# A mixture-of-experts stage on one core: one token tile's heads, then the other's, tokens in PSUM, routing in four parts

## What is computed

```
q = (xblk @ w_query).reshape(B, TOKEN_BLOCK, N_PEER_HEADS, 2, SUBKEY_DIM)      # 8 heads
s = einsum('bthpd,hpnd->bthpn', q, sub_keys)                                   # 2 x 128 keys
vals, idx = top_k(s, 16)
cand = vals[..., 0, :, None] + vals[..., 1, None, :]                           # 256 candidates
top_s, pos = top_k(cand, 16);  eidx = take_along_axis(cand_idx, pos)           # 16 of 16,384 experts
g = softmax(top_s)
h = einsum('btd,bthkd->bthk', xblk, expert_u[eidx])                            # a dot product of 1024
act = gelu(h) * g
y = einsum('bthk,bthkd->btd', act, expert_v[eidx])
```

## Time and profile before

| | |
|---|---|
| median of 3 runs | 3719.93 us (3708.38 to 3737.20) |
| the profiled execution | 3748.34 us, span 3746.5 us |
| busy in the span | PE 86%, PEld 69%, DVE 64%, ACT 39%, POOL 33% |
| POOL, 512 gathers each of u and v rows | 548.1 and 557.0 us busy, mean 1070 and 1088 ns |
| DVE, 512 dot products | 615.6 us busy, mean 1223 ns |
| HBM read | 932.73 MB, 249 GB/s over the span |
| expert stages (first to last u gather) | 284.9 to 1046.5 us and 1318.0 to 2084.9 us |

### The profile page before, as it was taken

How to read it: one execution, slowest core, us unless ns; L and a number is a source line. 1 busy time by engine, 2 the same in 40 slices (tenths; PEclk the granted TensorE clock), 3 DMA queues, 4 the chain that set the end, 5 groups by cost and what they waited for, 6 DMA issues and landing times. The chain is left out here.

```text
span 3746.5 us, 50783 instructions
## 1 busy us (share of the span) xinstructions
PE 3234.4 (86%) x18906; PEld 2588.8 (69%) x18906; DVE 2395.2 (64%) x4712; ACT 1457.6 (39%) x2874; POOL 1238.6 (33%) x1211
## 2 busy tenths in 40 slices
PE   6997788777789968887877799999999999999999
PEld 6894344443268944444432599888999998898899
DVE  6776666655557555655666565877666656767565
ACT  3642222222236412222221344565554444565543
POOL 1306677777623056776777200010000000000000
PEclk7998899988899988888988899999999999999999
DMA  7669999999976489999999654434355554334354
GB/s 294 212 222 349 380 366 384 382 365 358 331 280 207 141 335 360 368 373 361 377 357 361 228 183 152 147 119 141 130 170 185 183 183 141 130 135 135 131 185 163
DMA packets 258290, 937.14 MB, mean 250 GB/s; under 512 B 29312, under 2 KB 30720, under 8 KB 257792
## 3 DMA queue, kind: packets, MB, share of 16 engines
q0 software_dynamic: 161280, 587.27, 41.6%
q1 hardware_dynamic: 96768, 346.62, 27.1%
HBM read 932.73 MB, written 1.05 MB: 249 GB/s over the span
## 5 line engine op out<-in xcount | busy, mean ns | idle before, releaser
L695 PE MATMUL M<-rows,diag 128*128 128x512 f32 x2048 | 984.7, 638 | 350.9 <-ACT diag L919 257.8
L695 PEld LDWEIGHTS M<-rows,diag 128*128 128x128 f32 x2048 | 413.4, 205 | 882.1 <-issue 873.1
L268 DVE TENSOR_TENSOR w_low<-ring,w_high 128x1024 fp32r<-128x1024 f32 x560 | 685.9, 1228 | 415.0 <-ACT w_high L260 412.4
L1210 DVE CUSTOM_DVE_ANT_0 rows<-rows,attn 128x1024 f32<-128x1024 f32 x512 | 615.6, 1223 | 463.6 <-DMA rows<-in_expert_u_dram,expert 414.3
L287 PE MATMUL G<-x_high,w_high 128*128 128x256 f32 x2576 | 764.5, 297 | 50.0 <-DVE w_low L268 17.0
L290 PE MATMUL G<-x_high,w_low 128*128 128x256 f32 x2576 | 741.4, 288 | 0.0
L260 ACT ACTIVATE w_high<-ring 128x1024 fp32r<-128x1024 f32 x560 | 588.6, 1054 | 349.0 <-PE G L287 324.2
L289 PE MATMUL G<-x_low,w_high 128*128 128x256 f32 x2448 | 706.1, 288 | 0.0
L412 POOL DMA_INDIRECT rows<-in_expert_v_dram,expert x512 | 557.0, 1088 | 279.4 <-issue 129.6
L412 POOL DMA_INDIRECT rows<-in_expert_u_dram,expert x512 | 548.1, 1070 | 302.1 <-issue 154.5
L287 PEld LDWEIGHTS G<-x_high,w_high 128*128 128x128 f32 x2576 | 507.6, 197 | 63.6 <-issue 38.4
(11 more groups left out here) (360 smaller groups left out, 4779.8 us busy)
## 6 DMA issues: line engine op xcount, KB each, us to landing
ring<-in_stream_dram SPq DMA_DIRECT2D x654, 512.0 KB
ada_ring<-in_ada_stream_dram POOLq DMA_DIRECT2D x80, 512.0 KB, 4.9
rows<-in_ada_stream_dram POOLq DMA_DIRECT2D x16, 512.0 KB
rows<-in_expert_u_dram,expert POOLq DMA_INDIRECT x512
rows<-in_expert_v_dram,expert POOLq DMA_INDIRECT x512
const<-in_const_dram SPq DMA_DIRECT2D x1, 1096.5 KB, 11.2
x<-in_x_dram SPq DMA_DIRECT2D x1, 1024.0 KB, 5.4
out_dram<-x SPq DMA_DIRECT2D x8, 128.0 KB, 3.5
```

The lines of the kernel that those rows point to most:

```text
L268: dve.tensor_tensor(T["w_low"][:, part, :], T["ring"][:, place.slot(chunk, slots), :], T["w_high"][:, part, :].bitcast(F32), ALU.subtract) ...
L695: mm = pe.matmul(M[:, 2 * t + half, :], T["diag"][:, n % 4, :], T["v_rows"][:, n % SLOTS, half * 512:(half + 1) * 512], start=(h == 0 and ...
L1210: dve.tensor_tensor_reduce(row, row, T["x_tok"][:, t, :], 1.0, 0.0, ALU.mult, ALU.add, T["hid"][:, r, k:k + 1]).then_inc(sem["u_used"], 1)
```

## The change

It has six parts. Rounds now go `t, h = divmod(r, PEER_HEADS)`: all heads of tile 0, then all of tile 1. The tokens are transposed into PSUM and read from there: tile 0 in banks 2 and 3 of `M`, which tile 1's sum needs only from round 8 on, and tile 1 (after round 6) in two banks of `G`; the product becomes a `scalar_tensor_tensor` with an accumulator. `route` is cut into four parts behind products 2, 4, 6 and 8. `weigh` comes one product after its group's last in place of two. The queries of head r + 2 are done within round r, for r = 0 to 5. And y of tile 0 is finished in rounds 8 to 10.

```
-QUERY_AFTER = {(0, 5): 0, (0, 11): 1, (1, 1): 2, (1, 7): 3, (1, 12): 4}
-QUERY_COPIES = {(0, 2): 0, (0, 3): 1, (1, 1): 2, (1, 2): 3, (1, 3): 4}
+QUERY_AFTER = {0: 0, 2: 1, 4: 2, 6: 3, 8: 4}
+ROUTE_AFTER = {2: 0, 4: 1, 6: 2, 8: 3}
...
+    x_turned = (M[:, 2:4, :], G[:, G_XT % GB:G_XT % GB + 2, :])
+    x_tok = [tile.rearrange("p a b -> p (a b)") for tile in x_turned]
...
+            def turn_x(t):
+
+                if t:
+                    for n in range(2):
+                        bank_free(pe, g_free, G_XT + n)
+                for q in range(KD):
+                    mm = pe.transpose(x_turned[t][:, q // 4, q % 4 * P:(q % 4 + 1) * P],
+                                      xm[:, q, t * P:(t + 1) * P], ident)
+                    if t and q % 4 == 3:
+                        mm.then_inc(g_full, 1)
+                if t == 0:
+                    mm.then_inc(sem["x_turned"], 1)
...
             def add_experts(r):
 
-                h, t = divmod(r, TT)
+                t, h = divmod(r, PEER_HEADS)
...
-                    if h + 2 < PEER_HEADS and (t, k) in QUERY_AFTER:
-                        query_part(h + 2, QUERY_AFTER[t, k])
-                    if r == ROUNDS - 1 and k == SUB:
+                    if k in QUERY_AFTER and r + 2 < PEER_HEADS:
+                        query_part(r + 2, QUERY_AFTER[k])
+                    if r == PEER_HEADS and k == TOPK // 2:
                         turn_y(0)
+                if r == PEER_HEADS - 2:
+                    turn_x(1)
+                if opening and r == PEER_HEADS + 2:
+                    next_mean(0)
...
             for r in range(ROUNDS):
-                for at in range(r * TOPK, (r + 1) * TOPK, SUB):
-                    if at == ROUNDS * TOPK - SUB:
+                for j in range(TOPK // SUB):
+                    diagonals(r * TOPK + j * SUB)
+                    if r + 2 < PEER_HEADS and j in (1, 2):
+                        query_part(r + 2, 2 * j - 2)
+                        query_part(r + 2, 2 * j - 1)
+                    if j == 2 and r + 1 < ROUNDS:
+                        expert_softmax(r + 1)
+                    if r == PEER_HEADS and j == 0:
+                        copy_y(0)
+                    if r == PEER_HEADS + 2 and j == 0:
                         next_x(0)
...
+                if r + 2 < PEER_HEADS:
+                    query_part(r + 2, 4)
...
-                    dve.tensor_tensor_reduce(row, row, T["x_tok"][:, t, :], 1.0, 0.0, ALU.mult, ALU.add,
-                                             T["hid"][:, r, k:k + 1]).then_inc(sem["u_used"], 1)
-                    if k % SUB == 1 and n > SUB:
+                    dve.scalar_tensor_tensor(out=row, in0=row, scalar=1.0, in1=x_tok[t], op0=ALU.mult,
+                                             op1=ALU.mult, accum_out=T["hid"][:, r, k:k + 1]
+                                             ).then_inc(sem["u_used"], 1)
+                    if k % SUB == 0 and n:
                         weigh(n // SUB - 1)
-                    if k == SUB - 1 and r + 1 < ROUNDS:
-                        route(r + 1)
-                    if r == ROUNDS - 1 and k == TOPK - SUB - 1:
-                        add_y(0)
+                    if k in ROUTE_AFTER and r + 1 < ROUNDS:
+                        route_part(r + 1, ROUTE_AFTER[k])
```

More of the change, by code:

```diff
@@ L722, in _ @@
             first_queries()
-            for t in range(TT):
-                for half in range(2):
-                    g = G_XT + 2 * t + half
-                    bank_free(pe, g_free, g)
-                    for q in range(4):
-                        mm = pe.transpose(G[:, g % GB, q * P:(q + 1) * P],
-                                          xm[:, 4 * half + q, t * P:(t + 1) * P], ident)
-                    mm.then_inc(g_full, 1)
-            queries(1)
             pe.wait_ge(sem["std_ready"], F_NORM + 1)
             pe.wait_ge(sem["ada_read"], len(parts))
-            for h in range(PEER_HEADS):
-                for t in range(TT):
-                    add_experts(h * TT + t)
-            if opening:
-                next_mean(0)
+            pe.wait_ge(sem["o_ready"], HEADS)
+            turn_x(0)
+            queries(1)
+            for r in range(ROUNDS):
+                add_experts(r)
             turn_y(1)
@@ L891, in _ @@
                                    scale=scale1[:, 1, k:k + 1]).then_inc(sem["xm_ready"], 1)
-            def queries(h):
-                for j in range(5):
-                    query_part(h, j)
             def query_part(h, j):
@@ L935, in _ @@
                 first_queries(t)
[L936 to L939 removed]
+            for j in range(5):
+                query_part(1, j)
             expert_softmax(0)
             for r in range(ROUNDS):
[L942 to L952 removed]
+                for j in range(TOPK // SUB):
[8 more added lines that the diff above has]
+                    if r == PEER_HEADS + 2 and j == 0:
+                        next_x(0)
+                if r + 2 < PEER_HEADS:
+                    query_part(r + 2, 4)
                 if opening and r == 4:
@@ L1151, in route, with route_part @@
             def route(r):
-                h, t = divmod(r, TT)
-                evacuated(dve, g_free, g_scores(h, t))
+                for part in range(4):
+                    route_part(r, part)
+            def route_part(r, part):
+                t, h = divmod(r, PEER_HEADS)
                 val, idx, idxf, rest = T["val"], T["idx"], T["idxf"], T["rest"]
-                for p in range(2):
+                cand, top, pos = T["cand"], T["top"][:, r, :], T["pos"]
+                if part < 2:
+                    p = part
+                    evacuated(dve, g_free, g_scores(h, t))
                     s = T["key_score"][:, h, (2 * t + p) * P:(2 * t + p + 1) * P]
@@ L1200, in products @@
             def products(r):
-                t = r % TT
+                t, h = divmod(r, PEER_HEADS)
                 if r == 0:
-                    for g in range(2 * TT):
-                        evacuated(dve, g_free, G_XT + g)
+                    dve.wait_ge(sem["x_turned"], 1)
+                if r == PEER_HEADS:
+                    dve.wait_ge(g_full, G_XT + 2)
                 for k in range(TOPK):
@@ L1253, in _ @@
             for r in range(ROUNDS):
-                if not opening and r == ROUNDS - 1:
+                if not opening and r == PEER_HEADS:
                     dve.wait_ge(nxt["par_loaded"], 16)
@@ L1258, in _ @@
                 products(r)
+                if r == PEER_HEADS + 1:
+                    add_y(0)
+                if not opening and r == PEER_HEADS + 2:
+                    next_low(0)
                 if opening and r == 2:
@@ L1261, in _ @@
             weigh(ROUNDS * TOPK // SUB - 1)
-            if not opening:
-                next_low(0)
             add_y(1)
@@ L2494, in program @@
             att = sb1("attn", KD * S)
-            T1["attn"], T1["x_tok"] = part(att, 0, KD, S), part(att, 0, TT, D)
+            T1["attn"] = part(att, 0, KD, S)
             gates = sb1("gates", 2 * KD * S)
```

87 lines of the change are left out of this document (39 added, 48 removed).

## The result

| | median us | lowest to highest | runs | profiled run, span | clock |
|---|---|---|---|---|---|
| before | 3716.8 | 3692.4 to 3742.6 | 9 | 3746.5 | 0.929 |
| changed | 3692.1 | 3687.6 to 3696.9 | 9 | 3690.8 | 0.943 |

The ratio is 0.9939 with a 95% interval of 0.9914 to 0.9964: about 23 us came, where 88 were forecast. The profiled run of the kernel before (3748.3 us) was 31.5 us above this median, so the spans differ by more (55.7 us) than the medians.

What follows compares the result with a forecast made beforehand. GpSimd's gather rounds were taken as the bound. Gains of 110.7 us in the last ten rounds, less 26.9 in the first six, plus 4.5 at the ends, gave 88 us: median 3632 us, range 3580 to 3705.

Steps and rivals of the forecast that it cites:

- rival B: GpSimd's gathers: the stretch stays, from their own descriptor writing or the product's output; gain 18 us, 3702 us; chance 0.14.
- Bound by GpSimd's rounds: Last ten rounds: GpSimd sets the pace, each round 39.9 us of gathers plus 4.5 of stretch and 3.2 of waits.
- The gathers stretch because of the second SBUF input, and x in PSUM removes it: Last ten rounds: gathers lengthen during dot products reading two SBUF tensors; with x in PSUM, 44.7 and 44.2 us go.
- Routing in four ... I leave 1.0 of 3.2 us a round: Last ten rounds: splitting the 10.5 us routing block and earlier weights cut GpSimd's waits from 3.2 to 1.0 us a round.
- the queries' loop: Rounds 0 to 5: late score copies delay VectorE's routing; a round lies between 46.7 and 54.3 us.
- Transfers next at 410 GB/s, 417.7 us: Last ten rounds: transfers become the bound, 40.9 us a round plus 1.0 of waits, 417.7 us for 319 gathers.
- Rival A: Last ten rounds: transfers sustain only 388 GB/s, not 410; 438.6 us for 319 gathers, gain 46 us, 3674 us; chance 0.17.
- Queries moved, 49 us a round: First six rounds: a head's query work within one round makes it 49 us, 305.3 us in all; 26.9 us lost.
- Rival C: Rounds 0 to 5: the loop through routing and score copies takes over, 60 us a round; 44 us slower, 3764; chance 0.09.
- C's sign: Rounds 0 to 5: in the profile after, VectorE would be idle before the first MAX8 of a round.
- Ends of the stage, 4.5 us: Tail of each expert stage: tile 0's squares or copies and half a mean square leave, about 2.3 us a layer.
- TensorE's clock at nothing: Last ten rounds: TensorE needs 27.5 us of 42 at 2.4 GHz, so clock switching was costed at nothing.

Runs made afterwards that it cites:

- v eight behind: Changed kernel with v gathers running eight behind the u gathers instead of four: 3597.8 us on chip 3 (ratio to before 0.9908), 3753.1 us on chip 4 (1.0107).

## Why the prediction was wrong

The median, 3692, lies inside the range, near its upper edge (3705) and rival B's number (3702). That is luck: B was not what happened, the forecast 88 us were 23, and two errors of opposite sign are in them, 66.6 us too much in the last ten rounds and 38.0 us too little in the first six.

**Bound by GpSimd's rounds:** right. Where signals were prompt (chip 3, v eight behind), 58 us more stretch made the last ten rounds 50 us longer, and the waits gave the rest (11.7 to 1.0 us).

**The gathers stretch because of the second SBUF input, and x in PSUM removes it:** right. 947 ns a gather, the stretch 45.1 to 2.2 us, dot products of 1.22 us; with x back in SBUF it returned on all three chips where that ran (56.6 to 59.3 us). By the inference of the Trainium skill (SBUF — State Buffer, Who interferes with whom) that stood behind rival B it should have stayed; the measurement decides, and B is refuted.

**"Routing in four ... I leave 1.0 of 3.2 us a round":** the step that failed. The waits rose to 5 us. I had put them down to routing's 10 us block and v slots that TensorE had not freed. In part they were late signals, and these grew from 47 own late waits to 76 as the gathers came faster. The two gains were added as if they were independent; on a chip with late signals they are nearly one sum that keeps its size: 61.6 us with x in PSUM, 65.9 with x in SBUF (chip 2). The last ten rounds are then 45 us each, not 41.9. On chip 5, without late signals, the waits are 13.6 us, 1.4 a round, near the 1.0 forecast. What makes the signals late stays open, and they are not all of the miss: they slow the kernel before too, and on chip 5 the change gives 41 us (3626.9 to 3586.2), still less than half of 88. The signs stood in the trace read for the prediction: the scores' matmuls of the earlier trace rows ended at 496.97 and their copy, one of those in the earlier trace rows, started at 505.05, and VectorE had 47 late waits for itself. I saw the late copies, priced them for the queries' loop and left them out of the v waits.

**Transfers next at 410 GB/s, 417.7 us:** right in kind and never reached on chip 1; on chip 5 it was 409.5 us at 409 GB/s. Rival A is refuted there: 410 GB/s is held for a whole stage, not only for 20 us.

**Queries moved, 49 us a round:** too dear. 305.3 us forecast, 286 to 289 in the six stages traced on chips with late signals and 269 on chip 5, against 278 to 296 of before. These are the first six rounds with all parts of the change; no run undoes the move alone, so its own cost isn't shown. The forecast counted the move alone here, and nothing of what x in PSUM, early weights and routing in four give in these rounds. Rival C did not come. With routing in a block a loop of its kind did (329 us, the kernel at 3817), but through weights and diagonals, not by the wait for scores that was named as C's sign.

**Ends of the stage, 4.5 us:** zero. From the last u gather to the last expert's matmul 18.9 and 18.8 us before, 22.1 and 16.4 after; 18.1 and 18.7, then 18.4 and 22.0 on chip 4.

**TensorE's clock at nothing:** no run speaks against it. The granted clock of the last ten rounds is 0.88 before and after on chip 1, and 1.00 on chip 5, where TensorE's longest wait for a diagonal is 1.9 us. With x in SBUF on chip 2 it is 0.97, and that kernel ties with the changed one at 0.87.

**Sum as measured** on chip 4, profile against profile: last ten rounds 36.1 us, first six -13, tails -3.6, the start of the first stage -3.1, the rest about zero: 16 us between spans of 3709.1 and 3693.4. On this chip the gain lies in the order, not in x in PSUM, which ties; undone one at a time on chip 2, early weights gave 20 us and routing in four 113. x in PSUM is worth 74 us on chip 3, where signals are prompt, and nothing measurable on chips 2 and 4.

## What to carry to other kernels

Stretch and waits in front of one engine need not be independent terms: ask what a faster issue does to the things that answer it, and test the sum by undoing one part. Look for an engine's wait for its own last instruction; it should be a few hundredths of a microsecond, and where it is microseconds, signals are late and every chain of short steps in that stage is mispriced. Before a gain of one per cent is put down to an edit, look at which chip ran it: the same kernel differed by 3% between chips, and the changed kernel with v gathers eight behind took 0.991 of the kernel before on one chip and 1.011 on another. Count the recorded updates of a semaphore, too: where they are fewer than the kernel makes, the profile's releasers ("remote", "issue") are partly guesses.

## What the runs showed of the hardware

- On chips 1, 2, 4 and 6 an instruction that waited for its own engine's last one started up to 5.5 us late in stretches with a gather each 1.25 us; on chips 3 and 5 none of some 750 such waits a kernel was over 0.04 us. The changed kernel took 3692 to 3704 us on the first kind and 3586 on the second.
- On the first kind of chip the traces hold 4,403 to 8,376 of the 16,640 updates of the gathers' semaphores, on the second 16,637 or more. Whether the recording delays the signals isn't shown.
- Sixteen transfer engines moved 409 GB/s over 409.5 us in gathers of 4 KB rows.
- A MEMSET of one number a partition between two gathers took 0.118 us, and the gathers kept their 1.25 us: the idle time ahead of the next one fell from 0.30 to 0.19 us.
